# Dense feed-forward gate and up: one 512-column matmul over the high weights in place of two of 256 columns

## The reference, cut to what matters

```python
h2 = _rms_norm(x, norm_ffn_g[l])                       # 256 x 1024
gu = h2 @ w_ffn_in[l]                                  # 1024 x (2 * 2816)
ff_gate, ff_up = gu[..., :D_FF], gu[..., D_FF:]
x = x + (jax.nn.silu(ff_gate) * ff_up) @ w_ffn_out[l]  # 2816 x 1024

def _swiglu(h, w_gate, w_up, w_down):                  # the second block's, dense
    return (jax.nn.silu(h @ w_gate) * (h @ w_up)) @ w_down
```

## Time and profile before

| | |
|---|---|
| three timed runs | 1926.85, 1928.45, 1929.61 us; median 1928.45 |
| profiled execution, span from first to last instruction | 1929.0 us (no other time of it is given) |
| TensorE matmul busy | 1893.1 us, 98% |
| VectorE, ScalarE, GpSimd busy | 1497.7, 1246.1, 392.1 us |
| first dense feed-forward, TensorE's stretch | about 277 to 467 us |
| second dense feed-forward | about 611 to 801 us |

### The profile page before, as it was taken

One profiled execution on the slowest core, in us unless ns is written; L12 is line 12 of the kernel. 1 busy time (PEld: TensorE's weight loads), 2 busy tenths in 40 slices (PEclk: granted clock), 3 DMA queues, 4 the chain that ended last, 5 costly groups with the idle time before them and its releaser, 6 DMA issues.

```text
span 1929.0 us, 27194 instructions
## 1 busy us (share of the span) xinstructions
PE 1893.1 (98%) x9923; PEld 1609.9 (83%) x9923; DVE 1497.7 (78%) x1589; ACT 1246.1 (65%) x1478; POOL 392.1 (20%) x204
## 2 busy tenths in 40 slices
PE   8999999999999999999899999999999999999997
PEld 6788889998888999878788888888888888888886
DVE  7745366666765656696599999999999999899998
ACT  5654444445644444464388888888888888888886
POOL 5856870002824000382430000000000000000000
PEclk9999999999999999999999999999999999999999
DMA  9434556664433766534399999999999999999994
GB/s 279 155 130 131 175 186 214 215 226 153 140 123 121 224 216 214 162 118 142 131 376 394 380 395 361 392 396 354 394 353 396 397 354 395 355 395 396 356 396 186
DMA packets 251400, 524.53 MB, mean 272 GB/s; under 512 B 10008, under 2 KB 58784, under 8 KB 251184
## 3 DMA queue, kind: packets, MB, share of 16 engines
q1 hardware_dynamic: 244000, 506.36, 73.5%
q10 hardware_dynamic: 5088, 10.03, 1.4%
q0 software_dynamic: 2224, 6.96, 1.1%
HBM read 508.12 MB, written 15.20 MB: 271 GB/s over the span
## 4 chain that ended last, share of the span: by engine, by line
PE 90%; DVE 5%; ACT 2%; issue 1%; POOL 1%; DMA 0%; DVEq 0%; SPq 0%; ACTq 0%
PE bank L703 27%; PE bank L705 27%; PE bank L704 27%; PE bank L1056 2%; PE bank L1228 1%; DVE w_lo_sb L1810 1%; PE bank L777 1%; PE bank L750 1%; ACT w_hi_sb L1365 1%; PE bank L756 1%; POOL w_lo_sb L639 1%; PE bank L1109 0%; PE bank L1107 0%; PE bank L911 0%; PE bank L888 0%
## 5 line engine op out<-in xcount | busy, mean ns | idle before, releaser
L1810 DVE TENSOR_TENSOR w_lo_sb<-arena,w_hi_sb 128x1024 fp32r<-128x1024 f32 x672 | 806.9, 1223 | 74.0 <-ACT w_hi_sb L1365 48.0
L1365 ACT ACTIVATE w_hi_sb<-arena 128x1024 fp32r<-128x1024 f32 x672 | 710.5, 1062 | 164.9 <-PE bank L705 164.4
L703 PE MATMUL bank<-w_hi_sb,left_hi_sb 128*128 128x512 f32 (+1 forms) x1424 | 563.8, 396 | 7.4 <-issue 2.9
L705 PE MATMUL bank<-w_hi_sb,left_lo_sb 128*128 128x512 f32 (+1 forms) x1424 | 552.7, 388 | 0.0
L704 PE MATMUL bank<-w_lo_sb,left_hi_sb 128*128 128x512 f32 (+1 forms) x1424 | 552.2, 388 | 0.0
L1385 ACT ACTIVATE w_hi_sb<-arena 128x1024 fp32r<-128x1024 f32 (+1 forms) x269 | 280.3, 1052 | 336.2 <-PE bank L705 325.2
L639 POOL TENSOR_TENSOR w_lo_sb<-arena,w_hi_sb 128x1024 fp32r<-128x1024 f32 (+1 forms) x134 | 342.9, 2579 | 566.1 <-ACT w_hi_sb L1385 565.6
L703 PEld LDWEIGHTS bank<-w_hi_sb,left_hi_sb 128*128 128x128 f32 x1424 | 268.3, 188 | 66.2 <-issue 6.4
L705 PEld LDWEIGHTS bank<-w_hi_sb,left_lo_sb 128*128 128x128 f32 x1424 | 268.0, 188 | 56.0
L704 PEld LDWEIGHTS bank<-w_lo_sb,left_hi_sb 128*128 128x128 f32 x1424 | 268.6, 189 | 52.4 <-issue 0.7
L1822 DVE TENSOR_TENSOR w_lo_sb<-arena,w_hi_sb 128x1024 fp32r<-128x1024 f32 x135 | 163.8, 1219 | 126.4 <-ACT w_hi_sb L1385 125.5
(11 more groups left out here) (326 smaller groups left out, 1622.4 us busy)
## 6 DMA issues: line engine op xcount, KB each, us to landing
arena<-in_moe_w_gate SPq DMA_DIRECT2D x112, 1024.0 KB, 7.0
arena<-in_moe_w_up SPq DMA_DIRECT2D x112, 1024.0 KB, 8.1
arena<-in_moe_w_down SPq DMA_DIRECT2D x112, 1024.0 KB, 7.6
arena<-in_w_in SPq DMA_DIRECT2D x45, 1024.0 KB, 5.1
arena<-in_w_ffn_in SPq DMA_DIRECT2D x22, 1024.0 KB, 6.2
arena<-in_w_out SPq DMA_DIRECT2D x12, 1024.0 KB, 5.0
arena<-in_w_ffn_out SPq DMA_DIRECT2D x11, 1024.0 KB, 4.9
arena<-in_dense_w_gate SPq DMA_DIRECT2D x11, 1024.0 KB, 5.9
```

The source lines that it names most:

```text
L703: pe.matmul(out, still[0], moving[0], start=start, stop=False)
L705: return pe.matmul(out, still[1], moving[0], start=False, stop=stop)
L1365: act.activation(expert_buffer(w_hi_sb, j), expert_piece(j % MOE_SUBS), ACT.Copy) \
L1810: dve.tensor_tensor(expert_buffer(w_lo_sb, j), expert_piece(j % MOE_SUBS), expert_buffer(w_hi_sb, j).bitcast(F32), ALU.subtract) \
```

## The change

The two arrays of the activations become one, `left_sb`, with all high halves before all low halves, so that one access pattern takes the high and the low half of a k-tile together (2 x 256 columns). For a gate or up piece each k-step is now two matmuls: high weights with both halves, 512 columns wide, into the two halves of a whole bank, and low weights with the high half, 256 columns, added to the bank's first half. A piece thus fills a bank of its own, and the four banks serve one unit instead of two. VectorE gets `add_halves`, two reductions per kind that add the two halves of a bank and write 256 values each to SBUF; the scalings read from there. TensorE waits, before gate u and before up u, for the adds of unit u-1 (in place of the wait for the hidden block u-2). In unit 0 the copy of the factor row moves behind the adds of the gate.

```diff
-        left_hi_sb, left_lo_sb = (sb(f"left_{n}_sb", KD * TOKENS, F32R) for n in ("hi", "lo"))
+        left_sb = sb("left_sb", 2 * KD * TOKENS, F32R)
...
-        left_hi, left_lo = tiles(left_hi_sb[:, :], KD), tiles(left_lo_sb[:, :], KD)
+        left_both = left_sb[:, :].rearrange("p (s k n) -> p s k n", s=2, k=KD)
+        left_hi, left_lo = left_both[:, 0, :, :], left_both[:, 1, :, :]
...
-        def ffn_bank(tag, u, kind):
-            return gemm_bank[(gemm_at[{"f1": "wo0", "f2": "wo0_0"}[tag]] + 2 * (u % 2) + kind) % 4]
+        def ffn_bank(tag, kind, i):
+            return gemm_bank[(gemm_at[{"f1": "wo0", "f2": "wo0_0"}[tag]] + 2 * kind + i) % 4]
...
-                    b = ffn_bank(tag, u, kind)
+                    sums = tiles(ffn_bank(tag, kind, i)[:, :])
...
-                        mm = three_passes(b[:, i * TOKENS:(i + 1) * TOKENS], [a[:, k, :] for a in w],
-                                          (left_hi[:, k, :], left_lo[:, k, :]), k == 0 and (u > 0 or i == 0), k == KD - 1 and (u > 0 or i == 1))
+                        pe.matmul(sums, w_hi[:, k, :], left_both[:, :, k, :], start=(k == 0), stop=False)
+                        mm = pe.matmul(sums[:, 0, :], w_lo[:, k, :], left_hi[:, k, :], start=False, stop=(k == KD - 1))
...
-                        if u >= 2:
-
-                            pe.wait_ge(sem(f"{tag}_hid"), u - 1)
+                        pe.wait_ge(sem(f"{tag}_{('gate', 'up')[kind]}_added"), u)
...
+                    def add_halves(to, kind, name):
+
+                        for i in range(2):
+                            ins = dve.tensor_reduce(tiles(to)[:, i, :], ffn_bank(tag, kind, i)[:, :].rearrange("p (s n) -> p n s", s=2),
+                                                    AX_X, ALU.add)
+                        ins.then_inc(sem(name), 1)
+                        dve.wait_ge(sem(name), u + 1)
+
                     lo_to(min(gate_end + BUFFERS, ffn_range[tag][1]))
+                    dve.wait_ge(sem("w_used"), gate_end)
+                    add_halves(f_gate[u % 2], 0, f"{tag}_gate_added")
                     if u == 0:
                         copy_out(f"row_{norm_tag}", 0, f_row, P, TOKENS)
-                    dve.wait_ge(sem("w_used"), gate_end)
-                    mul(tiles(f_gate[u % 2]), tiles(ffn_bank(tag, u, 0)[:, :]), row, "f_scaled")
+                    mul(tiles(f_gate[u % 2]), tiles(f_gate[u % 2]), row, "f_scaled")
                     lo_to(min(up_end + BUFFERS, ffn_range[tag][1]))
                     dve.wait_ge(sem("w_used"), up_end)
-                    mul(tiles(f_up), tiles(ffn_bank(tag, u, 1)[:, :]), row)
+                    add_halves(f_up, 1, f"{tag}_up_added")
+                    mul(tiles(f_up), tiles(f_up), row)
```

More of the change, by code:

```diff
@@ L980, in into_hidden @@
                 def into_hidden(kind, u, i, ks):
-                    b = ffn_bank(tag, u, kind)
+                    sums = tiles(ffn_bank(tag, kind, i)[:, :])
                     j = span[f"{tag}_{('gate', 'up')[kind]}{u}"][0] + i
                     pe.wait_ge(sem(lo_count[j][0]), lo_count[j][1])
-                    w = [buffer(a, j, KD, P) for a in (w_hi_sb, w_lo_sb)]
+                    w_hi, w_lo = (buffer(a, j, KD, P) for a in (w_hi_sb, w_lo_sb))
                     for k in ks:
```

## The result

The changed kernel takes 1932.02 us, the median of 21 runs (1930.21 to 1935.6), where the kernel before takes 1928.56 in 21 runs on the same chips: a ratio of 1.0016, with an interval of 1.001 to 1.0022. That is 3.5 us slower, where 1.3 us faster was forecast. The stated range (1922.0 to 1938.0) holds the time, but the sign is the other one, and the time lies 0.5 us above 1931.5, the end of the narrower range that the forecast gave for itself, a pair up to 0.353 and an add up to 0.85. By its size the difference lies just within the 0.2% that the forecast called no change. With 21 runs a side it can be told from no change all the same.

The account below looks back on a forecast made before the run. TensorE's matmul stream was taken as the bound. The first feed-forward, 4.6 saved less stalls of 2.7, 0.9, 1.5, loses 0.5 us; the second, with stalls 0.4, 0.9, 1.5, gains 1.8: 1.3 us gained, 1927.1 us, range 1922.0 to 1938.0.

Parts of the forecast that it names:

- The pair: Gate and up k-steps: one 512 and one 256 matmul take 0.347 us for 0.360, saving 4.6 us a feed-forward.
- the two seams: Width changes in the earlier trace: 256s right after a 512 take 0.115 us each, 512s right after a 256 0.232.
- the third rival: Saved pass gives back little: a pair is 0.3575, a feed-forward saves 0.9 instead of 4.6, time 1933.5 us; chance 0.10.
- wait at up 1: TensorE waits at unit 1's up piece for the adds of up 0: 0.9 us in each feed-forward.
- The waits: TensorE idles three times a feed-forward: 2.8, 0.9, 1.5 us in the first and 0.4, 0.9, 1.5 in the second.
- First seam: First feed-forward, from unit 0 to unit 1's gate: stall 2.8 us behind the gate adds, 2.7 of it new.
- second: Second feed-forward, same place before unit 1's gate: TensorE stalls 0.4 us for the gate adds.
- Last unit: Before the last down block of each feed-forward: TensorE waits 1.5 us for the hidden block.
- The adds: VectorE's four new reductions a unit: 0.69 us each, two without a wait between them 1.29.
- the second rival: Adds are slow, 1.22 us each from the read order, and VectorE decides: 16.6 us more, time 1943.7; chance 0.14.
- Middle units: Steady units: adds hidden, losing the second set of banks costs nothing, a unit lasts 16.6 us instead of 17.0.
- The base of the sum: Profiled span 1929.0 us taken as 0.55 above the 1928.45 median, so a span of 1927.7 became a time of 1927.1.

Follow-up runs that it names:

- twos: Changed kernel with the matmul widths alternating 512, 512, 256, 256 instead of at every matmul: 1929.62 us, ratio 1.0002 to the kernel before.
- three passes: Changed kernel's banks, adds and waits, but three 256-column matmuls a k-step as in the kernel before: 1936.37 us, ratio 1.0048.
- hybrid: Changed kernel with unit 0, up of unit 1 and unit 10 back to three matmuls in one bank without adds, banks dealt anew: 1925.54 us, ratio 0.9982.
- eights: Changed kernel with all eight 512-column matmuls of a weight piece ahead of its eight of 256: 1931.63 us, ratio 1.0014.
- adjacent halves: Changed kernel with high and low token halves of a k-step side by side, so the 512 moving columns are contiguous: 1930.74 us, ratio 1.0014.
- last unit back: Changed kernel with only unit 10 back to three passes into one bank without adds: 1931.02 us, ratio 1.0011.
- angles later: Changed kernel with VectorE's rotation angles moved from ahead of the first feed-forward into its unit 5: 1930.05 us, ratio 1.0004.

## Why the prediction was wrong

**The pair: the step that failed.** "So a pair lies between 0.340 ... and 0.353 ...; I take 0.347, the middle and also the sum of the two seams." It measured 0.3528, the upper end. A feed-forward saves 11 x 0.22 = 2.4 us in its k-steps instead of 4.6, and 0.3 of that goes again in down blocks that take 5.50 instead of 5.47, a term that the prediction put at nothing. Over both stages 4.9 us of the forecast gain are missing, and that by itself turns the sign: with the forecast saving the stages would be 0.9 us shorter, not 4.0 longer. The range of the pair was right and the point in it was not. The seams of the earlier trace rows show one change of width between long runs, and neither runs nor twos lose anything there (0.348). A stream that changes at every matmul is another thing, and no row of before showed it. Its end at 0.353 was made from the rows nearest in kind: a 512 behind a 256 at 0.232 and a steady 256 at 0.120. That this sum fits is in part luck: in the stream, 512s average 0.236 and 256s 0.117, so the long ones are dearer than the 0.232 of the sum, and the short ones are cheaper than steady ones.

The page "TensorE: Matmul & The Clock Gate" of the Trainium skill, section "Wait — 56ns, not 53.3ns?", gave the third rival. If its 2.5 ns were all that a matmul fewer saves, the pair would by this estimate be 0.3575 and the saving almost nothing. The measured saving of 0.007 lies between that (0.0025) and the forecast (0.013). Per matmul the kernel pays 0.013 in streams of one width, as the earlier trace rows say.

**The half clock: not foreseen.** The prediction has no term for the clock. Behind the wait in the first feed-forward TensorE runs some 3.4 us at the 1.2 GHz level. Eleven matmuls from 290.18 take 3.63 us, where at full clock they would take about 2.0. Of these 1.6 us about half was lost anyway, since the wait at up 1 (forecast 0.9, seen as 0.64 once the clock is full) disappears inside it. Unit 1's part shows what is left: +1.31 for a forecast +0.5. The five profiles with a seam as long as this one all have it; since a shorter pause elsewhere has it in some executions only, how often the changed kernel pays it over 21 runs isn't known.

**The waits: right.** First seam +2.5 for 2.7 forecast, second +0.6 for 0.4. Up 1 in the second feed-forward: unit 1 is 0.63 longer though its steps save 0.22, so 0.85 for 0.9. Last unit +1.43 for 1.5 in both. The last unit's wait is shown by taking it back alone, the start's by moving the angles. All six together come to 7.6 us for 7.9 forecast (2.5 + 0.6 + 2 x 0.85 + 2 x 1.43); at the old pitch, in the kernel with three passes, the stages grew by 6.9.

**The adds: right.** 0.683 for 0.69, two in 1.28. So the second rival (adds at 1.22) falls: two values 256 words apart are read at the same price as neighbours. Its own sum was also a little high: it puts 3.0 for two pairs of adds in the last unit's chain, where its 1.1 a pair gives 2.2, and it doesn't say what the rest is.

**Middle units: right.** No wait shows between unit 2 and unit 9, and the second pair of banks isn't missed there. The hybrid's missing waits say the same. A steady unit lasts 16.79 us (11.29 and 5.50), where 16.6 was forecast and the kernel before has 16.98.

**The base of the sum.** The prediction set the span 0.55 above the median and found nothing around it. Where span and time of one execution are both known, the time is 1.8 above the span (1932.08 and 1930.3; 1921.16 and 1919.3). The profiled execution of before was thus about 2.2 us above its median. That moves no term. It explains why the spans differ by 1.3 us only while the medians differ by 3.5 and the stages by 4.0.

Added up: the stages were forecast at -1.3 and came to +4.0. Of the 5.3 between, 4.9 are the pair and the down blocks, 0.7 the half clock beyond the wait that it covers, and -0.3 the waits.

With the measured pair the prediction's own sum gives about 1931.2 us. The down blocks (0.6) and the half clock (0.7), for which it had no term, bring that to the 1932 that was measured.

What stays open is why alternation at every matmul costs 0.005 us a k-step and repeats every three pairs. The layout of the moving columns and a fixed price per change of width were ruled out by runs; the weight loads in between were not tried.

## What to carry to other kernels

When a change merges passes, price the new stream in the order in which it will be issued, and treat an order that the trace doesn't show as its dearer end; then try a few orders, because grouping the widths in twos cost three lines here and brought back what the alternation lost. When a change adds work between a producer's last result and the reuse of its bank, look at the first and the last unit of the loop: the steady units hid the adds entirely and the edges lost 6.9 us. A new form can be kept out of those edge units, and that, with grouped widths, made a change that lost 3.5 us into one that gains 7 to 8. And where a wait is new, look at the granted clock behind it, in more than one profile: the same pause had half clock behind it in some executions and not in others.

## What the runs showed of the hardware

- A stream of fp32r matmuls with a weight load each, that alternates 512 and 256 columns, runs at 0.3528 us a pair. The same matmuls in twos run at 0.3480 and in eights at 0.3483. Three 256s take 0.3598.
- Moving columns taken from two blocks 2048 words apart cost TensorE nothing against contiguous ones (0.3528 both).
- In the five profiles in which the seam to unit 1 left TensorE without a start for 2.88 to 3.00 us, the granted clock fell to the 1.2 GHz level right behind or late in it, for some 3.4 us (the changed kernel, adjacent halves, eights, twos, last unit back). With 2.75 us (three passes) and with 0.97 (angles later) it stayed at 2.4 GHz there. The length alone doesn't decide it: a pause of 1.71 us, the same at two places in all ten profiles, was followed by half clock in four cases of twenty. So a wait can cost twice, and one profile doesn't show how often.
- A reduction of two values that lie 256 words apart in a PSUM bank costs 0.683 us for 512 values read, the same as values side by side in SBUF (0.686).
